# One-core Trainium2 kernel, experts stage: the down weights of experts 4 to 31 are issued from ScalarE's own DMA queue, the up weights stay on SyncE's

## What is computed

```python
def hier_moe(h, w_rg, b_rg, w_re, b_re, w1e, w3e, w2e):
    ...
    cw = jnp.sum(jax.nn.one_hot(flat_idx, N_EXPERTS, dtype=f32) * wts[..., None], axis=1)
    out = jnp.zeros_like(t)
    for e in range(N_EXPERTS):
        he = jax.nn.silu(t @ w1e[e]) * (t @ w3e[e])
        out = out + cw[:, e:e + 1] * (he @ w2e[e])
```

## Time and profile before

| what | us |
|---|---|
| median of 3 runs (2733.32 to 2736.6) | 2734.15 |
| the profiled execution | 2730.52 |
| its span in the profile | 2728.7 |
| stage of the experts up to its last `down` product, in the profile | about 2368 to 2682 |

### The profile page before, as it was taken

How to read it: one execution, slowest core, us unless ns; L and a number is a source line. 1 busy time by engine, 2 the same in 40 slices (tenths; PEclk the granted TensorE clock), 3 DMA queues, 4 the chain that set the end, 5 groups by cost and what they waited for, 6 DMA issues and landing times. The chain is left out here.

```text
span 2728.7 us, 38511 instructions
## 1 busy us (share of the span) xinstructions
PE 2528.1 (93%) x15170; PEld 1857.7 (68%) x15170; DVE 1148.0 (42%) x1593; ACT 948.1 (35%) x1364; POOL 1000.2 (37%) x495
## 2 busy tenths in 40 slices
PE   7999998999999899999899999989998998599996
PEld 5776776788877667777678887768487686333334
DVE  5443522566663622342256664351754414311113
ACT  4443432444432333243244443252523323111112
POOL 5221531444457323152144446743122532223330
PEclk9999999999999989999999999989999999699998
DMA  3111331322256211132132226522001121699992
GB/s 130 70 47 31 108 108 40 100 92 92 79 201 229 77 62 46 35 112 101 49 99 99 92 77 210 193 91 100 1 3 49 62 77 64 270 400 364 360 371 103
DMA packets 76280, 333.86 MB, mean 122 GB/s; under 512 B 17113, under 2 KB 21209, under 8 KB 51801
## 3 DMA queue, kind: packets, MB, share of 16 engines
q1 hardware_dynamic: 62336, 313.98, 32.0%
q0 software_dynamic: 13824, 18.19, 1.9%
HBM read 372.67 MB, written 16.78 MB: 143 GB/s over the span
## 5 line engine op out<-in xcount | busy, mean ns | idle before, releaser
L227 PE MATMUL bank<-dense_s_hi,dense_w_hi 128*128 128x512 f32 x672 | 267.1, 398 | 12.8 <-POOL dense_w_lo L702 6.7
L229 PE MATMUL bank<-dense_s_hi,dense_w_lo 128*128 128x512 f32 x672 | 261.8, 390 | 0.0
L228 PE MATMUL bank<-dense_s_lo,dense_w_hi 128*128 128x512 f32 x672 | 261.8, 390 | 0.0
L702 POOL TENSOR_TENSOR dense_w_lo<-weights,dense_w_hi 128x1024 fp32r<-128x1024 f32 x77 | 199.1, 2586 | 93.6 <-ACT dense_w_hi L671 90.6
L1497 DVE TENSOR_TENSOR hidden<-up_y 128x512 f32 x44 | 158.2, 3595 | 64.6 <-ACT up_y L1461 64.0
L229 PE MATMUL bank<-xn_r,weights_r 128*128 128x512 f32 x448 | 176.2, 393 | 0.0
L1858 DVE SCALAR_TENSOR_TENSOR xn<-mix,xn 128x1024 f32<-128x1024 f32 x64 | 113.8, 1779 | 115.7 <-DMA mix<-in_modulation 105.1
L227 PEld LDWEIGHTS bank<-dense_s_hi,dense_w_hi 128*128 128x128 f32 x672 | 126.0, 188 | 53.5 <-POOL dense_w_lo L702 15.3
L3104 PE MATMUL bank<-moe_weights,mix 128*64 128x512 f32 x320 | 147.2, 612 | 7.1 <-DMA experts_more_up<-in_experts_up,moe_more_up 7.1
L1474 POOL TENSOR_TENSOR up_w_lo<-weights,up_w_hi 128x2048 fp32r<-128x2048 f32 x22 | 101.5, 4616 | 126.8 <-ACT up_w_hi L1449 126.8
L227 PE MATMUL bank<-xn_r,mix_r 128*128 128x512 f32 x352 | 141.8, 403 | 5.5 <-DVE up_xn_lo_r L345 5.4
(11 more groups left out here) (714 smaller groups left out, 6138.1 us busy)
## 6 DMA issues: line engine op xcount, KB each, us to landing
weights<-in_w_up SPq DMA_DIRECT2D x44, 1024.0 KB, 4.8
moe_weights<-in_experts_up SPq DMA_DIRECT2D x40, 1024.0 KB, 14.7
mix<-in_modulation SPq DMA_DIRECT2D x64, 512.0 KB, 5.0
weights<-in_w_xattn SPq DMA_DIRECT2D x24, 1024.0 KB, 4.9
weights<-in_experts_up SPq DMA_DIRECT2D x24, 1024.0 KB, 9.2
weights<-in_w_down SPq DMA_DIRECT2D x44, 512.0 KB, 3.9
moe_weights<-in_experts_down SPq DMA_DIRECT2D x40, 512.0 KB, 10.4
weights<-in_w_attn SPq DMA_DIRECT2D x8, 1536.0 KB, 6.4
```

The lines of the kernel that those rows point to most:

```text
L227: nc.tensor.matmul(out, left.hi, right.hi, start=first, stop=False)
L228: nc.tensor.matmul(out, left.hi, right.lo, start=False, stop=False)
L229: return nc.tensor.matmul(out, left.lo, right.hi, start=False, stop=last)
L702: nc.gpsimd.tensor_tensor(w[b].lo[:, :], units.rows(b, 0, D, 0, D), w[b].hi[:, :], ALU.subtract).then_inc(w_split, 1)
```

## The change

The loop of SyncE issues only the up weights. The down weights of expert e + 4 are issued by ScalarE, behind its copy of the result of the step that holds expert e, once the second count of `down_done` of that step is there.

```diff
             for e in range(4, EXPERTS):
                 sp.wait_ge(up_done, main_step[e - 4] + 1)
                 moe.load_up(sp, e)
-                sp.wait_ge(down_done, 2 * main_step[e - 4] + 2)
-                moe.load_down(sp, e)
...
                 nc.scalar.activation(out[n % 2][:, 0:T], g.bank[5][:, :], ACT.Copy).then_inc(out_read_act, 1)
+                for e in range(EXPERTS - 4):
+                    if main_step[e] == n:
+                        act.wait_ge(down_done, 2 * n + 2)
+                        moe.load_down(act, e + 4)
```

## The result

The changed kernel takes 2791.67 us (median of 4 runs, 2786.88 to 2794.33) against 2733.74 us for the kernel before (median of 4). The ratio is 1.0212, with a 95% interval of 1.0200 to 1.0225: 58 us slower. The forecast was 2760.4 us in a range of 2731 to 2778. The direction and the place were right; the size was above the range by 14 us, and 31 us above the forecast.

The account below looks back on a forecast made before the run. Bytes bound the experts' start, then TensorE with waits for up weights. 5.1 + 10.0 + 3.3 + 8.5 - 0.7 = +26.2 us on the median of 2734.15 gave 2760.4 us, range 2731 to 2778.

Parts of the forecast that it names:

- What bounds the stage: Experts' stage: bytes bound its first part, then TensorE; it waits for more tiles' gathered up weights and main up weights.
- Part 1, the start: Steps 1 to 4: later gather for step 2 against vanished main up waits, +5.1 us (0.9 to 9.1).
- The 2.0 us for the second half of that `up`: `up` of step 2: its second half waits for another 1 MB, 2 us (0 to 4).
- Part 2, groups 1 to 6: Critical gather lands later: +10.0 us (4.0 to 21.0) in groups 2 to 6, +3.3 (2.0 to 5.5) in group 1.
- high bound: Groups' gather delay: one more transfer ahead (1.3 us) plus a third queue taking a fifth of turns (2.1): 4.2 us.
- ScalarE's 1 MB is gone for part of the time: Group 2: reason for taking a gather delay of 2.0 us, nearer the low end of 0.8 to 4.2.
- Part 3, the clock: Slow TensorE clock behind long waits in six groups, one paying already: 5 x 1.7 = +8.5 us (0 to 8.5).
- The dividing line between 1.64 and 2.0 us: TensorE waits in the groups: the length above which a wait costs 1.7 us of slow clock.
- Part 4: SyncE and ScalarE issuing costs 0; the third wait for main up weights (0.76) goes: -0.7 us.
- That only the sequencer's time is saved, and so nothing changes: Skill's rule on SyncE's issuing: sum would be 0; the no-change rival says 2729 to 2739 us, chance 0.15.
- Faster, if the gathers keep their pace: GpSimd's queue served as before, step 2's gather still at about 2399: -7.0 us, 2727.2, chance 0.10.
- ScalarE was not held: Rival: ScalarE's issues stop while its queue is full, silu late in seven groups: +35 on top, 2795, chance 0.05.

Follow-up runs that it names:

- GpSimd's new order: Changed kernel, GpSimd issuing more up weights' gathers first, more down weights and token rows behind: 2746.49 us, ratio 1.0055; the same edit on the kernel before: 2730.64 us.
- the first experiment: Changed kernel with down weights back on SyncE's queue, up weights still issued early, so one hardware queue: 2757.2 us, ratio 1.0088.
- the run with the third queue alone: Changed kernel with SyncE's old waits for down kept, so up weights are issued as before and down weights stay on ScalarE's queue: 2750.73 us, ratio 1.0057.
- the first pause: Early up weights, one hardware queue, more up gathers first; SyncE holds expert 5 behind step 0's down products: 2721.93 us, against 2727.04 without that hold.

## Why the prediction was right or wrong

**What bounds the stage: right.** Of all weights TensorE waits for the gathered up weights and no others, at the places that were named: before step 2 and once in each of groups 1 to 6; group 7 is free.

**Part 1, the start: right in size.** The wait before step 2 was forecast as 0.8 + 9.3 = 10.1 us and is 11.29. The waits for main up weights are gone, as forecast. `up(4)` is 8.4 us later; with the 1.7 us of slow clock that stood behind it before, that is +6.7 against +5.1, within 0.9 to 9.1. The sharing of three loaded queues, which no row had shown, was right as well: from 2404 to 2408 us SyncE's, GpSimd's and ScalarE's queues moved about 2 : 2 : 1 in bytes, at equal numbers of packets.

```profile
q1 hardware_dynamic: 85, 0.70, 41.9%
q0 software_dynamic: 91, 0.65, 39.0%
q10 hardware_dynamic: 87, 0.33, 20.3%
```

One term was right by luck. The 2.0 us for the second half of that `up` were to be waiting for its bytes; the wait was 0.54 us, and the other 2.2 us by which the 32 products took longer (9.79 us against 7.08) are slow clock, which no term had priced here.

**Part 2, groups 1 to 6: the step that failed.** The delay of the critical gather was put at 2.0 us with a high bound of 4.2, so that waits of 3.3 us came out. They are 10.58, 6.80, 8.21, 7.37, 9.08 and 8.57, in sum 50.6 us. Against the 6.3 us of before that is +44.3, where 10.0 + 3.3 = 13.3 had been written; the high ends gave 26.5. In groups 2 to 6 alone it is 40.0 against 6.3, so 6.7 us a group where 2.0 had been written. The gathers say the same: they took 13.5 to 15.7 us there against 6.8 to 8.7 before, on the mean 6.7 us more.

The mechanism was the right one, and stood in the same paragraph ("its packets wait in turn behind SyncE's"), but the price was not worked out from it. I scaled a whole landing time (8.3 / 0.8) and added one transfer at the distance at which GpSimd issues them. What should have been counted are turns. In the changed kernel the three queues moved these packets in 5 us:

```profile
q1 hardware_dynamic: 173, 1.28, 61.4%
q10 hardware_dynamic: 166, 0.61, 30.1%
q0 software_dynamic: 170, 0.16, 9.4%
```

That is, as an estimate that spreads the packets evenly, 170 / 16 = 10.6 turns on each DMA engine in 5 us, 0.47 us a turn. A gather of 128 rows is then 8 turns, 3.8 us. In group 1 four of GpSimd's transfers were issued between 2438 and 2442 us: scatter, more down weights, token rows and the critical gather. They took:

```profile
moe_pair_rows<-memn,moe_pair POOLq DMA_INDIRECT x1, 9.3
xn<-in_experts_down,moe_more_down POOLq DMA_INDIRECT x1, 12.4
stds<-moe_rows,moe_token POOLq DMA_INDIRECT x1, 15.3
experts_more_up<-in_experts_up,moe_more_up POOLq DMA_INDIRECT x1, 17.2
```

With the issue times (2438.15, 2439.46, 2440.80, 2442.10) they landed at 2447.4, 2451.9, 2456.1 and 2459.3 us, so 4.5, 4.2 and 3.2 us apart, about a full pass of 8 turns for each. In groups 2 to 6 the same landings are 2.1 to 4.4 us apart. In group 2 of the kernel before the first three took the following, and the fourth 8.3 us:

```profile
moe_pair_rows<-memn,moe_pair POOLq DMA_INDIRECT x1, 7.8
xn<-in_experts_down,moe_more_down POOLq DMA_INDIRECT x1, 8.8
square<-moe_rows,moe_token POOLq DMA_INDIRECT x1, 9.4
```

They landed at 2474.9, 2477.2, 2479.1 and 2479.3: the last within 0.2 us of the third, since it went through in the pause of SyncE's queue. The high bound missed that without the pause the whole pass of every transfer ahead is paid. The run with GpSimd's new order shows it from the other side: with two transfers fewer ahead the critical gather of groups 2 to 6, in the same three-queue traffic, took 8.1 to 9.5 us. Group 1, where that edit left 9.59 of the 10.58 us, was priced as one more group of the same kind (+3.3 us); in that run it was the backlog of real transfers, and the prediction has no term for it.

The second omission is how long ScalarE's queue is loaded. "ScalarE's 1 MB is gone for part of the time" was counted in bytes at full speed. By turns its 256 packets last 16 turns, 7.5 us. The four transfers of step 3k, another 2 MB, are issued before TensorE is through with its wait (at 2448.57 in group 1, with the wait over at 2459.47), and the working on group 2 did not count them.

**Part 3, the clock: right in kind, small by a third.** All six waits were followed by the lower clock. The six `up`s took 9.00 to 9.96 us, in sum 57.4; at 7.09 us, with 1.7 us for the one that was slow before, they would have taken 44.2. That is +13.1 us against +8.5: these waits cost 1.9 to 2.9 us of clock each, where 1.7 had been read from one of 2 us. The dividing line between 1.64 and 2.0 us does not hold either. In the first experiment the products behind a wait of 2.86 us took 7.09 us, and in the run with the third queue alone those behind one of 1.90 us took 8.78.

**Part 4: right.** SyncE and ScalarE cost nothing (for ScalarE's hold the run with its waits alone, ratio 1.0005; for the issues only the profile), and the third wait for main up weights is gone (-0.8 us).

**Sum.** 6.7 + 44.3 + 13.1 - 0.8 = +63.3 us, the measured lengthening of the stage in the two profiles. Against the forecast of 26.2 us 37.1 are missing in the profiles (31 between the medians): 31.0 are the term of part 2, 4.6 the clock, 1.6 the start.

**The rivals.** That only the sequencer's time is saved, and so nothing changes, is the one that the Trainium skill, page "DMA: Bandwidth & Descriptors", section "Issuing engines are not separate DMA queues", would have given. The issue times of the trace (four transfers in 1.8 us) agree that this time was not the bound; the 46 us in the groups are what it leaves out. "Faster, if the gathers keep their pace" failed at the point where it was to be decided: the gather for step 2 landed at 2410, not at 2399. ScalarE was not held.

**What stays open.** Group 1 keeps a long wait in four kernels with a third queue and up rows of 8 KB (9.6, 10.6, 19.8 and 21.5 us), and has none with rows of 4 KB. In three of them (all but the changed kernel) a real transfer of the start was still ahead of the critical gather by the profile; in the changed kernel the last one had landed at 2438.5, with token rows behind it until 2441.7, just before the gather's issue at 2442.10. That this backlog is the cause was read from the profiles; no run moved those transfers alone out of the way. That the edits of GpSimd's order and of the packet size gained nothing on the kernel before is read from the profiles: with the new order other waits took the place of the old ones, and with the small packets the same waits stayed. No run tested either reading. And the first pause is worth 5 us on one chip, while `up(5)` came 3.2 us sooner with it in that pair of profiles; the rest was not traced.

## What to carry to other kernels

Before a transfer is moved to another queue or issued earlier, look for the small transfer that slips through the pauses of the big ones, and count its price in turns: packets ahead of it on its own queue, times one packet of every other queue that is loaded. A pause of a queue that looks like waste can be what keeps another queue's latency short, so early issue pays only once the small transfer has been put to the front of its own queue: here the same early up weights cost 24 us without that, gained 3 to 5 us with it, hardly more than the noise, and 10 to 12 us when the first pause was kept besides.

## What the runs showed of the hardware

- Loaded queues got equal numbers of packets, not of bytes: 555 and 552 in 8 us with two, 173, 166 and 170 in 5 us with three. A queue with rows of 4 KB got half the bytes of one with rows of 8 KB (0.84 MB against 1.70 with two queues, 0.73 against 1.46 with three).
- The size of other queues' packets sets a small gather's latency while these queues have no pause. Cutting 8 KB rows into 4 KB rows, with the bytes and places unchanged, took the critical gathers of groups 2 to 6 from 13.5 to 15.7 us down to 9.0 to 11.4 us, and 42 us off the kernel. On the kernel before, with its pauses, the same cut changed nothing (ratio 1.0007).
- A gather that moves almost no bytes is not cheap: with three queues loaded GpSimd's transfers of 128 rows landed 2.1 to 4.5 us apart.
- TensorE's clock was at its lower level behind every wait of 6.8 us and more in the changed kernel (0.51 granted in the 6 us behind the one of 10.58 us), which cost 1.9 to 2.9 us each time. The cost did not follow the length of the wait: waits of 2.81 and 3.66 us in two of the runs cost 2.9 and 3.0 us, one of 1.90 us cost 1.7, and one of 2.86 us cost none.
